# Second-layer expert biases as a dense product per token, in place of bias products in each expert job

## The reference

```
logits = h @ router_w + router_b
top_v, top_e = top_k(logits, 4);  gates = softmax(top_v)
per expert block: hid = x @ w1[e] + b1[e];  act = clamped SwiGLU(hid)
                  yb  = act @ w2[e] + b2[e]
y[token] += yb * gate        # four experts of 32 per token
out = rmsnorm(x + y, final_g)
```

## Time and profile before

| | us |
|---|---|
| median of 3 runs | 2142.43 (2141.09 to 2143.94) |
| the profiled execution | 2144.7 |
| its span, first to last instruction | 2143.0 |
| PE busy in it | 1999.7 (93%) |
| DVE busy | 1622.1 (76%) |
| ACT busy | 1314.2 (61%) |
| DMA | 506.40 MB, mean 236 GB/s |

### The profile page before, as it was taken

One profiled execution on the slowest core, in us unless ns is written; L12 is line 12 of the kernel. 1 busy time (PEld: TensorE's weight loads), 2 busy tenths in 40 slices (PEclk: granted clock), 3 DMA queues, 4 the chain that ended last, 5 costly groups with the idle time before them and its releaser, 6 DMA issues. The chain is left out here.

```text
span 2143.0 us, 40176 instructions
## 1 busy us (share of the span) xinstructions
PE 1999.7 (93%) x11184; PEld 1716.0 (80%) x11185; DVE 1622.1 (76%) x2205; ACT 1314.2 (61%) x1896; POOL 639.1 (30%) x743
## 2 busy tenths in 40 slices
PE   7999978788985999999999999999999999999993
PEld 6887867676874979889798898978898888978882
DVE  5343166895656978889888898889898898988985
ACT  5221244663444766867767676677777676776765
POOL 3100000320234232524425244244324253342521
PEclk9999989999986999999999999999999999999997
DMA  5222120004245988989899898989898898988988
GB/s 187 58 79 69 42 96 1 11 21 144 89 151 188 366 283 275 317 266 370 264 323 310 274 362 259 340 298 371 268 345 291 292 339 264 355 281 301 333 258 308
DMA packets 264158, 506.40 MB, mean 236 GB/s; under 512 B 37708, under 2 KB 38732, under 8 KB 263778
## 3 DMA queue, kind: packets, MB, share of 16 engines
q1 hardware_dynamic: 242984, 457.79, 61.5%
q0 software_dynamic: 21120, 47.90, 8.8%
HBM read 466.38 MB, written 39.22 MB: 236 GB/s over the span
## 5 line engine op out<-in xcount | busy, mean ns | idle before, releaser
L1841 DVE TENSOR_TENSOR wlo<-raw,whi 128x1024 fp32r<-128x1024 f32 x774 | 950.3, 1251 | 74.3 <-ACT whi L1320 71.7
L1320 ACT ACTIVATE whi<-raw 128x1024 fp32r<-128x1024 f32 x775 | 844.6, 1116 | 159.4 <-PE ps L1008 104.0
L1006 PE MATMUL ps<-xT,whi 128*128 128x320 f32 x1920 | 502.2, 348 | 0.6
L1008 PE MATMUL ps<-xT,wlo 128*128 128x160 f32 x1920 | 454.9, 237 | 0.0
L1008 PEld LDWEIGHTS ps<-xT,wlo 128*128 128x128 f32 x1920 | 367.6, 191 | 0.6
L1006 PEld LDWEIGHTS ps<-xT,whi 128*128 128x128 f32 x1920 | 361.5, 188 | 4.1 <-ACT y L1355 3.5
L640 PE MATMUL ps<-whi,xT 128*128 128x512 f32 x544 | 217.5, 400 | 0.0
L642 PE MATMUL ps<-whi,xT 128*128 128x512 f32 x544 | 214.2, 394 | 0.0
L641 PE MATMUL ps<-wlo,xT 128*128 128x512 f32 x544 | 213.6, 393 | 0.0
L640 PE MATMUL ps<-whi,aT 128*128 128x512 f32 x512 | 210.5, 411 | 0.3 <-DVE aTl L1902 0.3
L642 PE MATMUL ps<-whi,aTl 128*128 128x512 f32 x512 | 200.9, 392 | 0.0
(11 more groups left out here) (311 smaller groups left out, 3577.0 us busy)
## 6 DMA issues: line engine op xcount, KB each, us to landing
raw<-in_w SPq DMA_DIRECT2D x780, 512.0 KB, 9.2
raw<-in_w_in SPq DMA_DIRECT2D x16, 512.0 KB, 4.8
xs<-in_x SPq DMA_DIRECT2D x8, 512.0 KB, 10.2
raw<-in_w_out SPq DMA_DIRECT2D x8, 512.0 KB, 3.7
mix<-in_x SPq DMA_DIRECT2D x8, 512.0 KB, 4.2
acc_d<-mix SPq DMA_DIRECT2D x8, 512.0 KB, 5.1
h_d<-h SPq DMA_DIRECT2D x8, 512.0 KB, 2.6
mix<-acc_d SPq DMA_DIRECT2D x8, 512.0 KB, 7.7
```

The source lines that it names most:

```text
L1006: pe.matmul(o2, wh[:, a, cols], xT2[:, :, k, 0:JOB_T], start=q == 0 and a == 0, stop=False, skip_group_check=True)
L1008: m = pe.matmul(o, wl[:, a, cols], xT2[:, 0, k, 0:JOB_T], start=False, stop=q == QUARTERS - 1 and a == 1, skip_group_check=True)
L1320: act.activation(parted(slot(whis, s)), paired(raw_slot(s), s), ACT.Copy).then_inc(split_hi, 1)
L1841: dve.tensor_tensor(parted(slot(wlos, s)), paired(raw_slot(s), s), parted(slot(whis, s).bitcast(F32)), ALU.subtract).then_inc(split_lo, 1)
```

## The change

Jobs lose their second bias product, the load of its rows and the waits on it; the first product of a unit 4 or 5 now opens the bank itself. In exchange each tile of tokens gets a dense product in the router's pipeline: the gates of all 32 experts (zero where not picked), three times side by side, are transposed, rounded and multiplied with a constant block of bias rows (high, low, high), and the result is added to `mix` before it is stored to `acc_d`.

```diff
-                        if q == 0:
-                            pe.matmul(o, (ones2, ones1)[b][:, 0:n], brow[:, bias:bias + UNIT], start=True, stop=False)
+                        if q == 0 and c < 4:
+                            pe.matmul(o, ones2[:, 0:n], brow[:, c * UNIT:(c + 1) * UNIT], start=True, stop=False)
```

New on PE, with its place in the loop of steps:

```diff
+            def gates_turn(t):
+                pe.wait_ge(gates_set, t + 1)
+                if t > 0:
+                    pe.wait_ge(b2_added, 2 * t)
+                pe.transpose(ps[0:3 * NE, 1, 0:P], gates[:, :, :].rearrange("p a e -> p (a e)"),
+                             ident[:, :]).then_inc(gates_turned, 1)
+            def b2_prod(t, part):
+                if part == 0:
+                    pe.wait_ge(gT_lo, t + 1)
+                else:
+                    pe.wait_ge(b2_added, 2 * t + 1)
+                pe.matmul(ps[:, 1, :], gT[:, :], b2s[:, UNIT * part:UNIT * (part + 1)], start=True, stop=True).then_inc(b2_done, 1)
...
                     if 0 <= i - 1 < NT:
                         h2_turn(i - 1, half)
+                    if half == 0 and 0 <= i - 4:
+                        b2_prod(i - 4, 1)
+                    if half == 0 and 0 <= i - 3:
+                        gates_turn(i - 3)
+                    if half == 1 and 0 <= i - 3:
+                        if i == 3:
+                            pe.wait_ge(b2s_in, 48)
+                            pe.wait_ge(gT_zero, 1)
+                        b2_prod(i - 3, 0)
                 if 0 <= i - 2:
                     ranks(i - 2)
```

New on DVE: a product in `place`, and two functions, with their place in the loop:

```diff
+                dve.scalar_tensor_tensor(out=gates[:, :, :], in0=gall[:, :].unsqueeze(1).broadcast_to([P, 3, NE]),
+                                         scalar=grec[:, 0:1], in1=picked[:, :].unsqueeze(1).broadcast_to([P, 3, NE]),
+                                         op0=ALU.mult, op1=ALU.mult).then_inc(gates_set, 1)
+            def gates_lo(t):
+                dve.wait_ge(gT_hi, t + 1)
+                dve.tensor_tensor(gT[2 * NE:3 * NE, :], ps[2 * NE:3 * NE, 1, 0:P], gT[2 * NE:3 * NE, :].bitcast(F32),
+                                  ALU.subtract).then_inc(gT_lo, 1)
+            def b2_add(t, part):
+                dve.wait_ge(b2_done, 2 * t + part + 1)
+                if part == 0:
+                    dve.wait_ge(sq2, t + 1)
+                cols = slice(UNIT * part, UNIT * (part + 1))
+                dve.tensor_tensor(mix[:, t, cols], ps[:, 1, :], mix[:, t, cols], ALU.add).then_inc(b2_added, 1)
...
                     if 0 <= i - 1 < NT:
                         h2_lo_part(i - 1, half)
+                    if half == 0 and 0 <= i - 4:
+                        b2_add(i - 4, 1)
+                    if half == 0 and 0 <= i - 3:
+                        gates_lo(i - 3)
+                    if half == 1 and 0 <= i - 3:
+                        b2_add(i - 3, 0)
```

More of the change, by code:

```diff
@@ L187, in build @@
     bcolT = at("bcolT", B + 64 * KB, [P, 2, BTILES, NE])
+    gT = at("gT", B + 64 * KB, [P, P], F32R)
+    gates = at("gates", B + 64.5 * KB, [P, 3, NE])
+    gall = at("gall", B + 65 * KB, [P, NE])
     R = [B + 72.5 * KB]
@@ L199, in build @@
     junk0 = at("junk0", R[0], [P, D])
-    brow = rest("brow", [P, BW], F32R)
+    brow = rest("brow", [P, 2 * FF], F32R)
+    b2s = rest("b2s", [P, D], F32R)
     grow = rest("grow", [P, D])
@@ L283, in sem @@
             return ctx.enter_context(nc.semaphore(name))
-        x_in = [sem(f"x_in{t}") for t in range(NT)]
+        tile_in = [sem(f"tile_in{t}") for t in range(NT)]
         const_in, bias_in, bias_hi, bias_lo, bias_out, brow_in = (
@@ L327, in build @@
             sem(n) for n in ("tnext_in", "tnext_cast", "gathered", "tcur_set"))
[L328 removed]
+        brow1_in, b2s_in, gT_zero = sem("brow1_in"), sem("b2s_in"), sem("gT_zero")
+        gates_set, gates_turned, gT_hi, gT_lo, b2_done, b2_added = (
+            sem(n) for n in ("gates_set", "gates_turned", "gT_hi", "gT_lo", "b2_done", "b2_added"))
         x_turned, xT_hi, xT_lo, y_zero, scattered, jobs_over = (
@@ L537, in _ @@
             sp.wait_ge(brow_zero, 1)
-            sp.dma_start(brow[0:2, :].bitcast(F32), brow_d[NE]).then_inc(brow_in, 16)
+            sp.dma_start(brow[0:2, :].bitcast(F32), brow_d[NE, :, 0:2 * FF]).then_inc(brow_in, 16)
+            for i, low in enumerate((0, 1, 0)):
+                sp.dma_start(b2s[NE * i:NE * (i + 1), :].bitcast(F32), brow_d[0:NE, low, 2 * FF:BW]).then_inc(b2s_in, 16)
             for n in range(2, 8):
@@ L601, in _ @@
                 third_unit(q)
+            for t in range(4, NT):
+                first_sum(t)
             sp.wait_ge(jobs_set, 1)
@@ L620, in _ @@
                         sp.dma_start(raw_slot(s), src).then_inc(slot_in(s), 16)
[L621 to L626, removed]
             sp.wait_ge(jobs_over, 1)
             for t in range(NT):
-                sp.dma_start(mix[:, t, :], acc_d[t * P:(t + 1) * P, :]).then_inc(fin_in[t], 16)
+                sp.dma_start(mix[:, t, :], acc_d[t * P:(t + 1) * P, :]).then_inc(tile_in[t], 16)
             for t in range(NT):
@@ L946, in _ @@
                       jobr[:, :, :].rearrange("p a b -> p (a b)"), start=True, stop=True).then_inc(job_sum, 1)
+            b2_prod(NT - 2, 1)
+            gates_turn(NT - 1)
+            for part in range(2):
+                b2_prod(NT - 1, part)
             pe.wait_ge(b1r_in, 16)
@@ L1286, in gate, with gates_hi @@
                 act.activation(gexp[:, :], top[:, 0:TOPK], ACT.Exp, bias=ntop[:, 0:1],
-                               accum_out=gden[:, 0:1]).then_inc(gate_exp, 1)
+                               accum_out=gden[:, 0:1])
+                act.activation(gall[:, :], logit[:, :], ACT.Exp, bias=ntop[:, 0:1]).then_inc(gate_exp, 1)
+            def gates_hi(t):
+                act.wait_ge(gates_turned, t + 1)
+                if t == 0:
+                    act.wait_ge(gT_zero, 1)
+                else:
+                    act.wait_ge(b2_done, 2 * t)
+                act.activation(gT[0:3 * NE, :], ps[0:3 * NE, 1, 0:P], ACT.Copy).then_inc(gT_hi, 1)
             def h2_hi_part(t, half):
@@ L1393, in _ @@
                 jsplit(0, s)
+            gates_hi(NT - 1)
+            for i in range(2):
+                act.wait_ge(acc_out[i], 64)
             act.wait_ge(jobs_set, 1)
@@ L1835, in _ @@
             total = dve.value_load(jobt[0:1, 0, JT_W - 1:JT_W], min_val=0, max_val=JOBS)
+            b2_add(NT - 2, 1)
+            gates_lo(NT - 1)
+            for part in range(2):
+                b2_add(NT - 1, part)
             def jsplit(j, s):
@@ L2169, in _ @@
             pool.wait_ge(bcur_set, 1)
+            for i in range(2):
+                pool.wait_ge(acc_out[i], 64)
             with pool.Fori(0, JOBS, 1) as j:
```

62 lines of the change are left out of this document (33 added, 29 removed).

## The result

The kernel after took 2147.34 us in the median of 19 runs, the one before 2143.03 us in 19 runs on the same chip. The ratio is 1.0021, with a 95% interval of 1.0014 to 1.0027: 4.3 us slower, just at the edge of what a measurement of this kernel can tell from no change. (One run of the kernel after took 2505.87 us at a mean granted clock of 0.739, where the others have 0.968 to 0.969, and is in no ratio.) The forecast was 7.2 us slower, at 2149.6. The profiled execution took 2147.1 us, with a span of 2145.5, where the one before had 2144.7 and 2143.0.

A forecast was written before the change was run, and what follows sets the result against it. PE's own rate was taken to bound the jobs and the router's pipeline. Terms -21.5 + 15.0 + 6.0 + 7.7 = +7.2 us gave 2149.6 us; the forecast's own range was 2145 to 2155, the overall range 2139 to 2158.

The forecast's parts named there:

- bias products in jobs: Jobs: 94 products removed from PE at 0.23 us each, 21.5 us less, with 15 as the lower end.
- wait in `gates_turn`, four steps: Router steps 4 to 7: next half of the output projection 3.75 us later each, 15.0 us more; bounds 13 to 17.
- clock behind it: Router steps 4 to 7: a clock fall in each at 1.5 us, 6 us more; bounds 0 and 10.
- the pipeline's end: Router steps 8 and 9, one serial chain: added waits and work cost 7.7 us more; bounds 5 and 10.
- first three jobs, beyond their products: Jobs: only the removed products counted; work after the job table put at 0, 2 us at most.
- Rival 3: Jobs: DVE or DMA becomes the bound in narrow jobs; with half the 21.5 lost, +18, 2160 us; chance 0.07.
- The order on two queues: Steps 4 to 7: PE's `gates_turn` waits for DVE's add queued behind `choose`; 3.75 us later, PE idle 3.1.
- The cover on DVE: Router steps' second part: DVE's additions of 0.9 come out of its 1.22 us wait for PE, 0.3 left.
- Rival 2: Steps 4 to 7: the add is done in time, only the tail is paid; -15.5, 2127 us; chance 0.12.
- Rival 1: Steps 4 to 7: the wait is there but the clock stays up; +1.2, 2143.6 us; chance 0.22.
- so strict a reading: Router steps: an engine busy four fifths of each step would stay at the upper clock level; prediction argued against it.
- the logits' wait on `place`: Pipeline's end: logits(6) wait for `place(5)`, +2.1 us; an add, `place(6)` and its product precede logits(7), +2.15.

The follow-up runs named there:

- e1: Kernel before without the down-projection's bias products and their load, second biases left out of the result: 2120.58 us, ratio 0.9906.
- e3: Kernel after with thirteen unread 512-column products on PE ahead of the wait in `gates_turn`, steps 4 to 7: 2137.52 us, ratio 0.998.
- e2: Kernel after with the second bias product ahead of the logits on PE and its add ahead of `choose` on DVE: 2123.55 us, ratio 0.9913.
- e9: e6 with SP's stores of tiles 4 to 7 moved behind the first turned tokens: 2123.92 us, ratio 0.9915.
- e4: Kernel after with ACT's waits for the stores of `mix` moved behind its copies of the first tokens: 2145.2 us, ratio 1.0019.
- e5: e2 with the ranks of tiles 5 to 7 in bank 0, out of the logits' bank: 2123.34 us, ratio 0.9918.
- e7: e6 with `ranks(7)` and `place(7)` right behind `choose(7)`, tile 7's dense gates after, last adds between first weight splits: 2122.32 us, ratio 0.9913.
- e8: e7 with SP's first three loads of the third unit moved behind the wait for the job table: 2120.33 us, ratio 0.9897.
- e6: e5 plus e4's edit, moving ACT's waits for the stores of `mix` behind the first tokens: 2123.99 us, ratio 0.9918.

## Why the prediction came out nearly right

| term | predicted | measured |
|---|---|---|
| bias products in jobs | -21.5 | -21.0 (e1); -22.0 in the trace, being the -26.3 without the -4.3 below |
| wait in `gates_turn`, four steps | +15.0 | PE idle 3.15 in each; next half 3.74 late in step 5 |
| clock behind it | +6.0 | +6.9 by the halves; about 8 by e3 |
| the pipeline's end | +7.7 | +8.0 without the clock |
| first three jobs, beyond their products | 0 | -4.3 |
| ahead of the router | 0 | -1.2 (these two traces; inside the spread of the eleven) |
| sum | +7.2 | +4.3 by the medians, +2.5 by the spans |

**The jobs.** All of it holds: 68 instructions of the line, 35.63 and 53.23 us, PE busy throughout (predicted 35.7 and 53.3). Rival 3 is refuted by e1.

**The order on two queues.** This step carried the sign of the forecast: predicted 3.75 us and 3.1 of it idle, found 3.74 and 3.15, with DVE's add to `mix` as the releaser in all four steps. e2 shows that this is the cause. The cover on DVE was predicted to shrink from 1.22 to 0.3; it is 0.39. Rival 2 (the add is done in time) is what e2 makes true by an edit, and it gives 18 us less than before where that rival had 15.5 less.

**The clock.** I took four falls at 1.5 us, and four there are: behind each wait of 3.15 us, with the logits' narrow products ahead of it, the granted clock is at the lower level, for 3.4 us in three cases and for 6.8 in the other. By the lengths of the halves they cost 1.4, 2.6, 1.6 and 1.3 us, 6.9 in all. e3 keeps the delay and takes the falls away: its steps 4 to 6 are 5.9 us shorter than those of the kernel after (59.6 against 65.6), the first half of step 7 is as long (11.57 against 11.62), and the stretch from there to the first job, with the fourth fall in it, is 2.0 shorter (61.7 against 63.6). By the medians the two kernels are 8.4 apart, but by the traces 2.0 us of their difference lies in the jobs, where e3's third has no wait at all. So the term was 6.9 to some 8, and was under-sized by 1 to 2 us. Rival 1 (the wait is there but the clock stays up) is refuted for the kernel after; e3 shows what it would have been, -4.1 us and not the +1.2 that I gave it, as the first jobs were to give more than I had counted (below).

The Trainium skill (TensorE: Matmul & The Clock Gate, "What's actually happening"), taken as strictly as in the prediction, would have had PE at the upper level here. The windows show a clock of 0.92, 0.85 and 0.92 with PE busy in 17.8 of 21.4 us, 19.0 of 22.6 and 18.0 of 21.6: so strict a reading doesn't hold, and the measurement decides.

**The pipeline's end.** The size was right (7.7 against 8.0) but not its parts, and their agreement is luck. My terms led up to the last tile's first scatter. From the opening of step 7's second half that came 7.6 us later than before (26.2 to 33.8), of which 1.3 is the fourth fall of the clock: 6.3 against my 7.7. One of my terms there was wrong: logits(6) wait for the end of `place(5)` as I said (2.94 us, released by DVE's queue at line 1804), but they did not run at the lower clock. They take 2.0 us from 648.66 to DVE's first read at 650.67, where the prediction counted 1.9 before and 3.6 at the lower clock.

Behind the scatter four parts that I had priced at nothing add up to 1.7. The table's landing takes 1.9 us less (the last scatter is issued at 675.16, when the bulk transfers have drained), and the reading back 0.9 less. The gather took 6.6 us from its second part's issue to PE (684.60 to 691.16) where it had taken 3.7 before, 2.9 more. A store was in transit beside it, but e9 does not bear that out as the cause. And the stretch from the tokens to the job took 1.7 more, which is ACT's wait of 11.02 us for the stores of `mix`, as e4 shows; I had left 0 to 2 open for it. Finally e5 to e7 show that, with the early add in place, my terms for the logits' wait on `place` and for the adds ahead of the ranks aren't all on the path.

**The step that failed** is the one that put the first three jobs at their products alone. Counted from the first job's bias product, they took 129.5 us and not 135.6: 6.1 less, of which 8 products are 1.8. The third job's wait fell from 2.93 us to 1.76, and that job runs at a clock of 1.00 (35.62 us) where it had 0.93; these are 1.2 us for the wait and 2.6 by the earlier trace rows. In e1 the wait stays (2.98 us) and so does a fall, so their going belongs to the router's side of the change and not to the jobs'. The other changed kernels agree: the wait was 2.15 us (e4), 1.93 (e8), 1.62 (e9), 1.2 to 1.5 (e2, e5, e6, e7) and none in e3, with a fall behind it in e4 and e8 alone. Both before and after, the 16 DMA engines are at a share of 1.05 from 12 to 67 us behind the first job's opening. What ended the wait differs too: by the profile DVE's low parts of the weights in before and e1, ACT's scaling of the second job's results (`y`) in e2, e5, e6, e7 and e9. Why the first two jobs of the changed kernels are through sooner is not settled; no experiment isolated it.

That the sum came within 3 us of the result is partly luck: the falls of the clock cost 1 to 2 us more than I had, the first jobs gave 4.3 more, and the end of the pipeline came out even by parts that cancel.

**What stays open**: that wait; what sets the time of the gather; what PE waits for in the last 5 to 8 us ahead of the first job, where the profile names "issue" in some kernels and DVE's low parts in others, and why it is longest where bulk transfers are in transit (e8, e9); and whether e8's version is faster than e2's, both 18 to 22 us under the kernel before.

## What to carry to other kernels

When small work is added to a full pipeline, price the place in the two queues before the work: here work worth 0.3 us a step cost 5 to 6 us a step, as a bank had to be free for an instruction of PE and what freed it stood behind a long dependent chain on DVE. Look for the first moment at which the freeing instruction's inputs are ready and put it there; moving one call up on each of the two engines turned +4 us into -18. And a PE wait near 3 us should be booked with a fall of the clock behind it: in these traces each of the waits of 2.9 to 3.2 us in steps 4 to 7 and at the third job had one, at 1.3 to 2.6 us. If the wait can't be moved, filling it is worth the price (e3).

## What the runs showed of the hardware that I had not expected

- A wait of 3.15 us, with PE busy in four fifths of each step, was followed by the lower clock in all four steps. At the third job the clock fell behind waits of 2.93 to 2.98 us (before, e1), 2.15 (e4) and 1.93 (e8), but not behind 1.76 (after), 1.62 (e9) or less. Waits of 0.5 us in steps 4 to 6 were not followed by a fall (e2).
- One and the same wait may or may not be followed by a fall. The wait of 2.71 us ahead of the router stands in all eleven traces; in three of them (after, e4, e9) the clock fell and the half behind it took 4.8 us, in the others it took 3.4 to 3.5 at 1.00.
- Filling the wait of 3.15 us with products of no use (13 at a pitch near 0.23 us) made the kernel 8.4 us faster than leaving PE idle.
- Four small scatters needed 8.5 us from the first issue to the read-back when the bulk transfers had not drained by the last one (e7), and 6.3 us when they had (e8, and e2 with the same loads but later scatters).
